# A decoder layer on one core: half of the down-projection pieces of two groups as seven block products in place of eight

## The chip, the core and the metric

The kernel runs on one NeuronCore of a Trainium2 chip. The metric is the device time of one execution in microseconds (us), as the median of several runs.

## What is computed

One hybrid decoder layer on 256 tokens of width 2048, batch 1, all in float32: gated token mixers (latent attention and an RG-LRU recurrence), cross-attention to 256 memory rows, and a convolutional feed-forward block. The change touches the last block:

```python
h = rmsnorm(x, g_pre_ffn[l])
up = causal_dwconv(h @ w_up[l], w_fconv[l], b_fconv[l])
gate, val = jnp.split(up, 2, axis=-1)
x = x + rmsnorm((jax.nn.gelu(gate, approximate=True) * val) @ w_down[l], g_post_ffn[l])
```

`w_up` is 2048 x 11264, `w_down` is 5632 x 2048. The product with `w_down` is the down-projection.

## The kernel before

**Products of float32 by three terms.** Each operand of a large product is split into a high part (rounded to the matmul's format, `fp32r`) and a low part (what is left). A product is then high x high + low x high + high x low, three matmuls (`TERMS`), summed in PSUM. For the weights the split is made on the way: a *piece* of 1 MB (128 partitions x 2048 values) lands by DMA in one of four slots of `raw`; ScalarE copies it to `wsp[.., 0, ..]` (the high part, function `hi`, L1041 to L1054); VectorE subtracts that from `raw` and writes `wsp[.., 1, ..]` (the low part, function `lo`, L1533 to L1540); TensorE waits for the low part (`arrive`). SyncE issues the load of piece c when the low part of piece c-4, the last owner of the `raw` slot, is done (`piece`, L365). ScalarE writes the high part of piece c when TensorE has finished piece c-4, the last owner of the `wsp` slot. ScalarE and VectorE run two pieces ahead of TensorE (`LEAD = 2`): the program text of a phase handles pieces 2 to n+1, so the last two splits are those of the next phase.

**The feed-forward block** is done in three groups of the 44 feature tiles (`GROUPS = [(0, 16), (16, 16), (32, 12)]`). For each group first the up-projection (`PH_UP`), in rounds of two gate and two value tiles (`up_round`), four pieces a round. What TensorE makes there goes through a chain of small operations: ScalarE copies half of it out of PSUM (L1065), VectorE adds the other half (L1548), scales (L2081), two convolution steps (L2086, L2092), ScalarE applies bias and gelu (L1448, L1467), GpSimd multiplies gate and value into `HID` (L2303), ScalarE (L1474) and VectorE (L2122) split that into `hsp`.

Then the down-projection of the group (`PH_DN`, functions `dn_mm` and `dn_y`): one piece is one row tile k of `w_down`, 128 x 2048. TensorE multiplies it with both token halves m and four column quarters b, three terms each, so 24 matmuls of 128 x 512 a piece, into all eight PSUM banks (bank 4m + b). In the first two groups a phase has 16 pieces, 384 matmuls. At its end VectorE moves the eight banks into `y_tok` (L2141 a copy in group 0, L2143 an addition in group 1), and TensorE enters the next up-projection when the first four banks are free (`y_out`). The third group (12 pieces) ends with the norm and the output; it reads `x3_tok`, the residual, which lies in `big_a` from before the first group.

The order of work is written out by hand: each engine has its own program, and the semaphores join them.

## Time and profile before

| | us |
|---|---|
| median of 3 runs | 1735.39 (1735.25 to 1735.74) |
| profiled execution, first to last instruction (span) | 1732.8 |
| TensorE busy in the span | 1724.4 |
| VectorE busy | 1142.9 |
| ScalarE busy | 919.5 |
| GpSimd busy | 157.3 |

The span counts from the first to the last instruction; the time of a run is 2.6 us longer than the span of the profiled execution, for what lies around it. In the rows PE is TensorE's matmul, PEld its weight load, DVE VectorE, ACT ScalarE, POOL GpSimd, SP SyncE; L12 is line 12 of the kernel. The time of one matmul in a group is that of its own way through the pipeline; successive matmuls overlap, so what one adds to the time is the length of a stretch divided by the count.

### The profile page before, as it was taken

To read this page: it belongs to the slowest core of one execution; us is meant where nothing else is said; L and a number is where in the kernel's file an instruction comes from. 1 tells how busy PE (TensorE), PEld (TensorE's weight loads), DVE (VectorE), ACT (ScalarE), POOL (GpSimd) and SP (SyncE) were. 2 spreads that over 40 slices of the span, in tenths; PEclk is the share of its full clock that TensorE was granted. 3 is DMA by queue.
4 is the path that set the end of the run, shared out by engine and by line. 5 is a ranking of instruction groups with operands and counts; after the bars stand their busy time and mean duration, and the time that the engine had idled before them with its cause. 6 is when DMAs were issued, how large, how long until landed. Compare 5 with 4: busy or idle time off the path is not lost.

```text
span 1732.8 us, 25350 instructions
## 1 busy us (share of the span) xinstructions
PE 1724.4 (100%) x8968; PEld 1470.6 (85%) x8968; DVE 1142.9 (66%) x1437; ACT 919.5 (53%) x1175; POOL 157.3 (9%) x183
## 2 busy tenths in 40 slices
PE   9999999999999999999999999999999999999998
PEld 8888888888888888888888888888888888888886
DVE  7766665466788874446566677775467776467766
ACT  7656655443666763344456665553355555245553
POOL 0012210000334520000000000000000000000000
PEclk9999999999999999999999999999999999999999
DMA  9645556566566565556554465556456556545552
GB/s 340 200 141 156 156 196 234 190 237 195 157 193 188 170 242 192 192 187 243 195 177 172 137 194 185 180 179 231 155 185 194 184 181 237 174 151 188 194 213 103
DMA packets 214267, 330.09 MB, mean 190 GB/s; under 512 B 5696, under 2 KB 161984, under 8 KB 206784
## 3 DMA queue, kind: packets, MB, share of 16 engines
q1 hardware_dynamic: 208576, 318.53, 54.5%
q10 hardware_dynamic: 5632, 10.75, 1.7%
q8 instruction: 40, 0.66, 0.2%
q14 instruction: 19, 0.16, 0.0%
HBM read 327.16 MB, written 2.10 MB: 190 GB/s over the span
## 4 chain that ended last, share of the span: by engine, by line
PE 99%; DVE 0%; issue 0%; ACT 0%; DVEq 0%; POOL 0%; POOLq 0%
PE ps L506 51%; PE ps L569 40%; PE ps L522 3%; PE ps L781 1%; PE ps L709 1%; PE ps L631 1%; PE ps L620 0%; PE ps L601 0%; PE ps L738 0%; PE ps L714 0%; PE ps L731 0%; PE ps L625 0%; PE ps L739 0%; PE ps L869 0%; PE ps L853 0%; PE ps L595 0%
## 5 line engine op out<-in xcount | busy, mean ns | idle before, releaser
L1540 DVE TENSOR_TENSOR wsp<-raw,wsp 128x2048 fp32r<-128x2048 f32 (+2 forms) x303 | 671.7, 2235 | 326.3 <-ACT wsp L1054 323.1
L1054 ACT ACTIVATE wsp<-raw 128x2048 fp32r<-128x2048 f32 (+2 forms) x304 | 558.0, 1855 | 284.4 <-PE ps L569 278.1
L506 PE MATMUL ps<-asp,wsp 128*128 128x512 f32 x3064 | 542.4, 339 | 0.0
L506 PEld LDWEIGHTS ps<-asp,wsp 128*128 128x128 f32 x3064 | 469.8, 188 | 70.2 <-DVE asp L2001 0.3
L569 PE MATMUL ps<-wsp,hsp 128*128 128x512 f32 x2292 | 522.9, 389 | 0.0
L569 PEld LDWEIGHTS ps<-wsp,hsp 128*128 128x128 f32 x2292 | 430.0, 188 | 89.0
L506 PE MATMUL ps<-hsp,wsp 128*128 128x512 f32 (+1 forms) x1936 | 349.7, 340 | 0.0
L506 PEld LDWEIGHTS ps<-hsp,wsp 128*128 128x128 f32 x1936 | 297.5, 188 | 42.9
L569 PE MATMUL ps<-wsp,asp 128*128 128x512 f32 x768 | 175.6, 389 | 0.0
L1065 ACT ACTIVATE cr<-ps 128x256 f32<-128x256 f32 x185 | 69.2, 380 | 197.2 <-PE ps L506 180.8
L569 PEld LDWEIGHTS ps<-wsp,asp 128*128 128x128 f32 x768 | 144.0, 188 | 29.8
L2303 POOL TENSOR_TENSOR scr<-scr 128x256 f32<-128x256 f32 x44 | 34.2, 797 | 1003.9 <-DVE scr L2092 1003.9
L1448 ACT ACTIVATE scr<-scr,par 128x256 f32<-128x256 f32 x88 | 48.2, 595 | 60.8 <-DVE scr L2081 60.8
L1548 DVE TENSOR_TENSOR cr<-ps,cr 128x256 f32<-128x256 f32 x88 | 35.1, 418 | 44.4 <-ACT cr L1065 44.4
L2086 DVE SCALAR_TENSOR_TENSOR scr<-scr,par 128x255 f32<-128x255 f32 x88 | 42.5, 484 | 27.4 <-ACT scr L1448 27.2
L2284 POOL TENSOR_TENSOR scr<-scr 128x256 f32<-128x256 f32 x16 | 28.6, 1785 | 246.8 <-ACT scr L1245 246.8
L522 PE MATMUL ps<-wsp,asp 128*128 128x512 f32 (+1 forms) x256 | 47.5, 341 | 0.0
L1474 ACT ACTIVATE hsp<-scr 128x256 f32 (+1 forms) x44 | 18.4, 418 | 53.6 <-POOL scr L2303 53.6
L522 PEld LDWEIGHTS ps<-wsp,asp 128*128 128x128 f32 x256 | 40.0, 188 | 5.8
L2122 DVE TENSOR_TENSOR hsp<-scr,hsp 128x256 f32 (+1 forms) x44 | 18.8, 427 | 36.2 <-ACT hsp L1474 36.2
L1164 ACT ACTIVATE scr<-scr,st 128x128 f32<-128x128 f32 (+1 forms) x32 | 14.3, 449 | 48.3 <-DVE st L1722 48.3
L2092 DVE SCALAR_TENSOR_TENSOR scr<-scr,par 128x254 f32<-128x254 f32 x88 | 38.3, 476 | 0.1
(264 smaller groups left out, 935.6 us busy)
## 6 DMA issues: line engine op xcount, KB each, us to landing
raw<-in_w_up SPq DMA_DIRECT2D x88, 1024.0 KB, 5.6
raw<-in_w_in SPq DMA_DIRECT2D x64, 1024.0 KB, 5.4
raw<-in_w_down SPq DMA_DIRECT2D x44, 1024.0 KB, 5.4
raw<-in_w_in SPq DMA_DIRECT2D x32, 768.0 KB, 4.4
raw<-in_w_o_mla SPq DMA_DIRECT2D x16, 1024.0 KB, 5.0
raw<-in_w_o_lru SPq DMA_DIRECT2D x16, 1024.0 KB, 5.1
raw<-in_w_out SPq DMA_DIRECT2D x16, 1024.0 KB, 5.0
raw<-in_w_ukv SPq DMA_DIRECT2D x8, 1024.0 KB, 5.4
```

What stands on the lines that cost most here:

```text
L506: mm = pe.matmul(ps[:, bank, 0:w], lhs(part, k), x[:, 0:w], start=(f and part == 0), stop=(l and n == 1))
L522: mm = pe.matmul(o, x, r, start=(f and part == 0), stop=(l and n == 1))
L569: mm = pe.matmul(ps[:, bank, :], src[:, k, low * T + m * P:low * T + (m + 1) * P], wsp[:, c, part, cols], start=(first and t == 0), stop=( ...
L1054: act.activation(wsp[:, p0 % SLOTS, 0, 0:n], raw[:, p0 % SLOTS, 0:n], ACT.Copy).then_inc(hi_done, 1)
L1065: act.activation(cr[:, slot, :], ps[:, bank, T:2 * T], ACT.Copy, scale=scale).then_inc(cross_done, 1)
L1448: act.activation(UC[2 * v + e], UR[2 * v + e], ACT.Identity, scale=col(W_F + 2 * P, m), bias=col(B_F, m)).then_inc(up_bias, 1)
L1540: dve.tensor_tensor(wsp[:, slot, 1, 0:n], raw[:, slot, 0:n], wsp[:, slot, 0, 0:n].bitcast(F32), ALU.subtract).then_inc(lo_done, 1)
L1548: return dve.tensor_tensor(dst, ps[:, bank, 0:T], cr[:, slot, :], ALU.add)
L2086: own.mark(dve.scalar_tensor_tensor(out=buf[:, 1:T], in0=src[:, 0:T - 1], scalar=col(W_F + P, m), in1=buf[:, 1:T], op0=ALU.mult, op1=ALU.add))
L2092: dve.scalar_tensor_tensor(out=buf[:, 2:T], in0=src[:, 0:T - 2], scalar=col(W_F, m), in1=buf[:, 2:T], op0=ALU.mult, op1=ALU.add).then_inc( ...
L2284: own.mark(pool.tensor_tensor(IG[e], IG[e], XC[e], ALU.mult))
L2303: pool.tensor_tensor(HID[e], UC[e], UC[2 + e], ALU.mult).then_inc(hid_out, 1)
```

## The change

In the down-projections of the first two groups a piece is now two row tiles (k0, k1) by half of the columns (1024), that is four blocks in order: (k0, b0), (k0, b1), (k1, b0), (k1, b1), each 128 x 512. The phase is two halves h (columns 0 to 1023, then 1024 to 2047), each over the eight pairs of row tiles. Four of the eight pairs stay as they were: a "plain" piece, 24 matmuls. The other four are done by seven block products in place of eight (the Strassen-Winograd form). Each takes two pieces: a "first" piece, loaded by DMA, with three products (9 matmuls), and a "made" piece, not loaded but computed by VectorE from the first, whose four blocks are sums of the first's blocks, with four products (12 matmuls). `DN_HALF` is the order of the twelve pieces of a half.

On the other side four sums of hidden blocks (`forms`) are made for each such pair: GpSimd (`form_sums`) once in every second up round, then split by ScalarE (`form_high`) and VectorE (`form_low`). They lie over `big_a`, so the residual is saved to DRAM in the first group's second round and loaded back ahead of the third group.

The seven products accumulate in PSUM over the four pairs: `q1`, `q6`, `q7`, `q5` in four banks, and the plain ones in the other four, which also take what belongs to one output block alone. At the end of a half ScalarE copies `q1` out (`q1_keep`), VectorE combines the q banks into `y_tok` (`products_out`) and adds the plain banks (`plain_out`). The halves use the two sets of four banks in turn.

The third group is as before, but for a wait on the residual.

```diff
+DN_HALF = [("plain", 0), ("plain", 2), ("first", 1), ("made", 1), ("first", 3), ("made", 3),
+           ("plain", 4), ("first", 5), ("made", 5), ("first", 7), ("made", 7), ("plain", 6)]
...
 SyncE
+                if fn == 16:
+                    for c in range(24):
+                        kind, pair = DN_HALF[c % 12]
+                        if kind != "made":
+                            k, c0 = f0 + 2 * pair, (c // 12) * 1024
+                            piece(dn, 0, c, 2, 1024, w_dn[:, k:k + 2, c0:c0 + 1024])
...
 TensorE
+                        if at == 0 and h == 1:
+                            pe.wait_ge(dn_out, 16 * n + 4)
...
+                        if at == 2 and 2 * n + h:
+                            pe.wait_ge(dn_out, 16 * n + 8 * h)
...
+                        elif kind == "first":
+                            form_mm(q1, block(k0, 0), slot, 1, at == 2, at == 9)
+                            form_mm(dn_plain_bank(h, 0, 1), block(k1, 0), slot, 3, False, False)
+                            mm = form_mm(dn_plain_bank(h, 0, 0), form(pair, 3), slot, 2, False, False)
+                        else:
+                            form_mm(q5, form(pair, 1), slot, 0, at == 3, at == 10)
+                            form_mm(q7, form(pair, 0), slot, 1, at == 3, at == 10)
+                            form_mm(q6, form(pair, 2), slot, 2, at == 3, at == 10)
+                            mm = form_mm(dn_plain_bank(h, 1, 1), block(k1, 1), slot, 3, False, False)
...
 ScalarE
+                def made_high(c):
+                    slot = (dn.p0 + c) % SLOTS
+                    act.wait_ge(gemm_step, dn.g(0, dn.used[c - SLOTS]) if c >= SLOTS else dn.g0)
+                    act.wait_ge(sums_made, dn_sums(n, c) + 1)
+                    act.activation(wsp[:, slot, 0, :], raw[:, slot, :], ACT.Copy).then_inc(hi_done, 1)
...
 VectorE
+                def sums_two(c):
+                    dve.wait_ge(lo_done, dn.p(0, c) + 2 - SLOTS)
+                    dve.wait_ge(landed[(dn.p0 + c) % SLOTS], dn.landed(0, c))
+                    b12 = raw_blocks(c, 0).rearrange("p (a t) -> p a t", a=1).to_broadcast([P, 2, 512])
+                    own.mark(dve.tensor_tensor(raw_blocks(c + 1, 0, 2).rearrange("p (a t) -> p a t", a=2), b12,
+                                               raw_blocks(c, 1, 2).rearrange("p (a t) -> p a t", a=2), ALU.add))
+                def sums_rest(c):
+                    own.wait()
+                    own.link(dve.tensor_tensor(raw_blocks(c + 1, 2), raw_blocks(c + 1, 0), raw_blocks(c, 2), ALU.add))
+                    dve.tensor_tensor(raw_blocks(c + 1, 3), raw_blocks(c + 1, 2), raw_blocks(c, 3), ALU.add).then_inc(sums_made, 1)
...
+                if fn == 16:
+                    form_low(n, 3)
+                    for c in range(LEAD, 24 + LEAD):
+                        kinds = ["plain" if at >= 24 else DN_HALF[at % 12][0] for at in range(c, c + 2)]
+                        if c == LEAD:
+                            sums_two(c)
+                            sums_rest(c)
+                        if kinds[1] == "first":
+                            sums_two(c + 1)
+                        if c == 15:
+                            plain_out(0)
+                        if kinds[0] == "first":
+                            first_low(c)
+                        else:
+                            lo(dn, 0, c)
+                        if kinds[1] == "first":
+                            sums_rest(c + 1)
+                        if c in (13, 25):
+                            products_out(c // 24)
+                        if c == 25:
+                            plain_out(1)
```

How the change moves instructions, at two places. First VectorE at the start of the first down-projection, behind the last up round. Before (L1540 is the low part of a weight piece):

```order
L2122 TENSOR_TENSOR hsp<-scr,hsp 128x256
L351 REGISTER_ALU
L351 COMPARE_AND_BRANCH
L2144 UNCONDITIONAL_BRANCH
L2144 ISA
L1540 TENSOR_TENSOR wsp<-raw,wsp 128x2048 [waits hi_done]
L1538 REGISTER_ALU
L1540 TENSOR_TENSOR wsp<-raw,wsp 128x2048 [waits hi_done]
```

and now (L2213 is `form_low`, L2293, L2299 and L2300 are the weight sums, L2306 the low part of a first piece, L1681 that of a made or plain one):

```order
L2213 TENSOR_TENSOR forms<-scr,forms 128x4x128 [waits fm_hi]
L2293 TENSOR_TENSOR raw<-raw 128x1024 [waits landed2,lo_done]
L2299 TENSOR_TENSOR raw<-raw 128x512 [waits dve_self]
L2300 TENSOR_TENSOR raw<-raw 128x512 [waits dve_self]
L2306 TENSOR_TENSOR wsp<-raw,wsp 128x1536 [waits hi_done]
L2293 TENSOR_TENSOR raw<-raw 128x1024 [waits landed0,lo_done]
L1681 TENSOR_TENSOR wsp<-raw,wsp 128x2048 [waits hi_done]
```

Four operations now stand ahead of the low part of piece 2, and one more ahead of that of piece 3.

Second VectorE around the middle of that phase, between the halves (pieces 10 to 14; L2322 to L2330 are `products_out`):

```order
L1681 TENSOR_TENSOR wsp<-raw,wsp 128x2048 [waits hi_done] x3
L2293 TENSOR_TENSOR raw<-raw 128x1024 [waits landed2,lo_done]
L1681 TENSOR_TENSOR wsp<-raw,wsp 128x2048 [waits hi_done]
L2299 TENSOR_TENSOR raw<-raw 128x512 [waits dve_self]
L2300 TENSOR_TENSOR raw<-raw 128x512 [waits dve_self]
L2322 TENSOR_TENSOR scr<-cols_in,ps 128x512 [waits q1_out,gemm_step]
L2326 TENSOR_TENSOR cols_in<-scr,ps 128x512 [waits dn_out]
L2328 TENSOR_TENSOR cols_in<-ps,scr 128x512
L2330 TENSOR_TENSOR cols_in<-ps,cols_in 128x512 [waits dn_out]
```

and TensorE at the same place (L600 is a plain piece, L1016 a first or made one; the row with `dn_out` is the start of the second half, piece 12):

```order
L1016 MATMUL ps<-wsp,forms 128x512 [waits lo_done]
L1016 MATMUL ps<-wsp,forms 128x512 x8
L1016 MATMUL ps<-wsp,hsp 128x512 x3
L600 MATMUL ps<-wsp,hsp 128x512 [waits hid_lo,lo_done]
L600 MATMUL ps<-wsp,hsp 128x512 x23
L600 MATMUL ps<-wsp,hsp 128x512 [waits dn_out,hid_lo,lo_done]
L600 MATMUL ps<-wsp,hsp 128x512 x23
L600 MATMUL ps<-wsp,hsp 128x512 [waits hid_lo,lo_done]
L600 MATMUL ps<-wsp,hsp 128x512 x23
L1016 MATMUL ps<-wsp,hsp 128x512 [waits fm_lo,dn_out,hid_lo,lo_done]
```

TensorE's piece 12 now stands behind VectorE's fourth operation of `products_out`. Before there was no such wait inside a phase.

## Rows read from the trace of the kernel before

**Rows 1.** Busy time by stage: down 0, up 1, down 1 (stretches of the span)
```profile
core 0: us, PE busy (x) PEld busy (x) DVE busy (x) ACT busy (x) POOL busy (x), PEclk, DMA share, GB/s
...
1170.28:1257.32 87.04, 87.04 (x385) 72.09 (x385) 43.73 (x32) 32.29 (x21) 1.61 (x2) 1.00 0.54 194
1257.32:1437.47 180.15, 180.15 (x1025) 156.68 (x1025) 127.39 (x170) 96.92 (x123) 10.69 (x14) 1.00 0.57 186
1437.47:1524.52 87.05, 87.05 (x386) 72.10 (x385) 43.73 (x32) 32.29 (x21) 1.53 (x2) 1.00 0.54 194
```
**Rows 2.** The chain that ended last: start us, us, what
```profile
1170.28 87.04 PE ps L569 x384
1257.32 180.16 PE ps L506 x1024
1437.47 87.04 PE ps L569 x384
```
**Rows 3.** Groups of instructions of the first down-projection: xcount | busy, mean ns | idle before
```profile
L1540 DVE TENSOR_TENSOR wsp<-raw,wsp 128x2048 fp32r<-128x2048 f32 x16 | 36.1, 2289 | 38.2 <-ACT wsp L1054 38.2
L1054 ACT ACTIVATE wsp<-raw 128x2048 fp32r<-128x2048 f32 x16 | 30.0, 1911 | 47.7 <-PE ps L569 47.7
```
**Rows 4.** Timeline of its start: start us, us, what, [idle before <-releaser]
```profile
1173.99 1.61 POOL L2303 TENSOR_TENSOR scr<-scr 128x256 f32<-128x256 f32 x2 [20.91 <-DVE scr L2092]
...
1176.34 0.42 DVE L2122 TENSOR_TENSOR hsp<-scr,hsp 128x256 f32 x1 [0.27 <-ACT hsp L1474]
1178.08 8.90 DVE L1540 TENSOR_TENSOR wsp<-raw,wsp 128x2048 fp32r<-128x2048 f32 x4 [1.31 <-ACT wsp L1054]
```
**Rows 5.** VectorE groups over the whole span, shapes apart
```profile
L1540 DVE TENSOR_TENSOR wsp<-raw,wsp 128x1536 fp32r<-128x1536 f32 x32 | 55.9, 1765 | 15.4 <-ACT wsp L1054 15.3
...
L2143 DVE TENSOR_TENSOR cols_in<-cols_in,ps 128x512 f32<-128x512 f32 x15 | 10.0, 684 | 5.7 <-PE ps L569 5.5
...
L1772 DVE TENSOR_TENSOR hsp<-scr,hsp 128x512 fp32r<-128x512 f32 x8 | 5.5, 685 | 0.7 <-ACT hsp L1216 0.7
...
L1869 DVE TENSOR_TENSOR big_a<-big_a,scr 128x512 f32<-128x512 f32 x4 | 2.6, 685 | 0.0
...
L2062 DVE TENSOR_TENSOR wsp<-raw,wsp 128x1024 fp32r<-128x1024 f32 x2 | 2.4, 1216 | 0.0
```
**Rows 6.** ScalarE groups over the whole span, shapes apart
```profile
L1054 ACT ACTIVATE wsp<-raw 128x1536 fp32r<-128x1536 f32 x32 | 46.5, 1478 | 0.3
...
L1216 ACT ACTIVATE hsp<-scr 128x512 fp32r<-128x512 f32 x8 | 5.0, 631 | 14.0 <-DVE scr L1782 13.6 <-ACT scr L1207 0.4
```
**Rows 7.** GpSimd groups over the whole span, shapes apart
```profile
L2303 POOL TENSOR_TENSOR scr<-scr 128x256 f32<-128x256 f32 x44 | 34.2, 797 | 1003.9 <-DVE scr L2092 1003.9
...
L2262 POOL TENSOR_TENSOR scr<-scr,st 128x256 f32<-128x256 f32 x16 | 9.8, 614 | 0.0
...
L2262 POOL TENSOR_TENSOR scr<-scr,st 128x128 f32<-128x128 f32 x16 | 6.4, 400 | 91.9 <-DVE st L1726 91.4
```
**Rows 8.** Timeline of VectorE in the tail: two operations each of which waits for the last
```profile
1715.75 0.15 DVE L2184 TENSOR_SCALAR st<-st 128x1 f32<-128x1 f32 x1
...
1716.60 0.15 DVE L2169 RECIPROCAL st<-st 128x1 f32<-128x1 f32 x1
1716.80 0.22 DVE L2170 SCALAR_TENSOR_TENSOR st<-st 128x1 f32<-128x1 f32 x1
```
**Rows 9.** DMA issues: KB each, median us from issue to landing
```profile
raw<-in_w_up SPq DMA_DIRECT2D x88, 1024.0 KB, 5.6
...
raw<-in_w_down SPq DMA_DIRECT2D x44, 1024.0 KB, 5.4
...
raw<-in_w_o_mla SPq DMA_DIRECT2D x16, 1024.0 KB, 5.0
...
raw<-in_w_in SPq DMA_DIRECT2D x4, 576.0 KB, 7.5
```
**Rows 10.** The last stretches of the span, columns as in rows 1
```profile
1726.00:1728.00 2.00, 0.31 (x2) 0.30 (x2) 1.61 (x7) 0.77 (x3) 0.00 (x0) 1.00 0.00 0
1728.00:1730.00 2.00, 0.36 (x2) 0.00 (x0) 1.62 (x3) 0.38 (x1) 0.00 (x0) 0.94 0.63 234
1730.00:1732.00 2.00, 0.00 (x0) 0.00 (x0) 0.00 (x0) 0.00 (x0) 0.00 (x0) 0.50 0.88 291
```
**Rows 11.** Up round ahead of down 0, VectorE's splits: timeline
```profile
1155.58 4.49 DVE L1540 TENSOR_TENSOR wsp<-raw,wsp 128x2048 fp32r<-128x2048 f32 x2 [1.33 <-ACT wsp L1054]
...
1164.25 4.71 DVE L1540 TENSOR_TENSOR wsp<-raw,wsp 128x2048 fp32r<-128x2048 f32 x2 [0.42 <-ACT wsp L1054]
```

More of the change, by code:

```diff
@@ L75, with __init__ @@
 class Phase:
-    def __init__(self, after, trips, ends, crosses=True):
+    def __init__(self, after, trips, ends, crosses=True, made=()):
         self.trips, self.ends, self.n = trips, ends, len(ends)
@@ L96, in __init__ @@
         self.x_end = self.x0 + (self.tiles * trips if crosses else 0)
-        assert self.n % SLOTS == 0
+        self.made = (after.made if after else []) + [self.p0 + c for c in made]
+        assert self.n % SLOTS == 0 and (not made or trips == 1)
     def p(self, i, c):
@@ L111, in landed @@
     def landed(self, i, c):
-        return i * (16 * self.n // SLOTS) + 16 * ((self.p0 + c) // SLOTS + 1)
+        at = self.p0 + c
+        skipped = sum(q < at and q % SLOTS == at % SLOTS for q in self.made)
+        return i * (16 * self.n // SLOTS) + 16 * (at // SLOTS + 1 - skipped)
 class Tally:
@@ L152 @@
     PH_UP.append(Phase(_last, _count // 2, [0, 2, 0, 2]))
-    PH_DN.append(Phase(PH_UP[-1], _count // 4, [0] * 4))
+    if _count % 16 == 0:
+        PH_DN.append(Phase(PH_UP[-1], 1, [0] * 24, made=[c for c in range(24) if DN_HALF[c % 12][0] == "made"]))
+    else:
+        PH_DN.append(Phase(PH_UP[-1], _count // 4, [0] * 4))
     _last = PH_DN[-1]
@@ L237, in build @@
         HID = [s(12), s(13)]
+        FORM = s(8, 2)
+        A11, A21, A12, A22 = (scr[:, 12 * T + n * P:12 * T + (n + 1) * P] for n in range(4))
+        Q1_KEPT, V_SUM, W_SUM = s(14, 2), s(8, 2), cur[:, :]
         landed = [sem(f"landed{n}") for n in range(SLOTS)]
@@ L305, in build, with dn_sums, dn_plain_bank @@
         half = RANK + ROPE
+        def dn_sums(n, c):
+            return 8 * n + 4 * (c // 12) + [e for e in DN_HALF if e[0] == "made"].index(DN_HALF[c % 12])
+        def dn_plain_bank(h, m, b):
+            return 4 * h + 2 * m + b
         def load_cols(eng, n):
@@ L997, in _ @@
                 i, last_ks = dn.trips - 1, range(fn - 4, fn)
[L998 removed]
+                for cs in ((0,), (1,), (2, 3)):
                     for c in cs:
@@ new lines, in _ @@
+                        mm = dn_mm(c, k, 1, b, False, c == 3)
+                    mm.then_inc(dn_done, 1)
+                for h in range(2):
+                    if h:
+                        pe.wait_ge(y_out, 1)
+                    for c, k in enumerate(last_ks):
+                        for t, (part, low) in enumerate(TERMS):
+                            mm = pe.matmul(ps[:, 0 if h else 7, 0:T], hsp[:, k, low * T + P:low * T + 2 * P], wsp[:, c, part, LAST[h]],
+                                           start=(h == 1 and c == 0 and t == 0), stop=(c == 3 and t == 2))
+                    mm.then_inc(dn_done, 1)
@@ new lines, in plain_out @@
+                def plain_out(h):
+                    dve.wait_ge(dn_out, 16 * n + 8 * h + 4)
+                    if n:
+                        own.wait()
+                    for at, (m, b) in enumerate([(0, 0), (0, 1), (1, 0), (1, 1)]):
+                        if at == 3:
+                            dve.wait_ge(gemm_step, dn.g(0, dn.used[12 * h + 11]))
+                        else:
+                            dve.wait_ge(dn_done, 6 * n + 3 * h + at + 1)
+                        y = y_at(h, m, b)
+                        dve.tensor_tensor(y, y, ps[:, dn_plain_bank(h, m, b), :], ALU.add).then_inc(dn_out, 1)
@@ L2293, in _, with form_sums @@
             own.n, own.off = n0 + 6 * PH_LRU.trips, 0
-            for (f0, fn), up in zip(GROUPS, PH_UP):
+            def form_sums(n, pair):
+                pool.wait_ge(hid_out, pair * 4 + 16 * n + 4)
+                if not isinstance(pair, int) or 4 * n + pair:
+                    pool.wait_ge(fm_lo, pair + 4 * n)
+                f7_f5, f6, f3 = (FORM[:, a * P:b * P] for a, b in ((0, 2), (2, 3), (3, 4)))
+                both = scr[:, 12 * T:14 * T].rearrange("p (e t) -> p e t", e=2)
+                own.link(pool.tensor_tensor(f7_f5.rearrange("p (e t) -> p e t", e=2), both[:, 0, :].rearrange("p (e t) -> p e t", e=2),
+                                            both[:, :, P:2 * P], ALU.subtract))
+                own.link(pool.tensor_tensor(f6, FORM[:, P:2 * P], A11, ALU.subtract))
+                pool.tensor_tensor(f3, f6, A12, ALU.add).then_inc(fm_raw, 1)
+            n0 = own.n
+            for n, ((f0, fn), up) in enumerate(zip(GROUPS, PH_UP)):
                 def up_round(i):
```

244 lines of the change are left out of this document (181 added, 63 removed).

## The prediction

> **What bounds the kernel now.** I read the busy time by stage first, then the chain of waits, the groups of the stage, and its timeline. TensorE is busy without a gap through every stage of the feed-forward block, at a granted clock of 1.00, the 2.4 GHz level [rows 1]; the chain that ended last is its matmuls alone [rows 2]. A down-projection takes 87.04 us for 384 matmuls, so 0.2267 us each. VectorE is busy 43.7 of those 87 us, ScalarE 32.3, and both idle only because their `wsp` slot is still in use [rows 1, 3]. So a matmul taken away is worth its 0.2267 us as long as VectorE and ScalarE keep up.
>
> **What TensorE gains.** Per half, four pairs of row tiles go from 24 matmuls to 21. Two halves, two groups: 16 x 3 = 48 fewer, 360 in place of 384 a phase, all of the same shape. 48 x 0.2267 = 10.9 us; a phase needs 81.6 us. A plain piece takes 5.44 us, a first one (9) 2.04, a made one (12) 2.72.
>
> **What VectorE pays.** Prices from rows of the same shapes [rows 3, 5]: low part of 2048 columns 2.29 us, of 1536 1.77; 1024-column sum 1.22; a 512-column addition 0.684, from SBUF or PSUM alike. Of operations that don't wait for each other the next starts 0.065 us before the last one's end (four splits of 2.289 take 8.90 [rows 4]); one that waits for the last starts 0.04 after it [rows 8]. The broadcast operand of the 1024 sum has no row. Bounds: 0.61 us (half the plain row) and 2.29 (twice as many columns); I take the plain 1.22, the nearest.
> A pair costs VectorE 1.22 + 2 x 0.684 + 1.77 + 2.29 = 6.6 us while TensorE works 4.8 on it. Before, two row tiles cost it 4.6 against TensorE's 10.9. A half is four of these, four plain splits and 8 (group 0) or 12 (group 1) additions at its end: 26.6 + 9.2 + 5.5 or 8.2 = 41.3 or 44.0 us, against 40.8 of TensorE. VectorE goes from half idle to as loaded as TensorE, with only two pieces of lead to even out the order. That is the core of the forecast: the gain is eaten unless it never waits, and the order makes it wait.
>
> **The timeline of a phase**, t = 0 where TensorE begins it (1170.28).
> Start. Before, VectorE comes free of the last up round's chain at t = 6.5, starts the low part of piece 2 at 7.8 and ends it near 10.1 [rows 4], 0.8 us ahead of TensorE, which has pieces 0 and 1 until 10.9. Now GpSimd first makes the form sums behind its last product, which ends at 5.3 [rows 4]: 0.80 for 256 columns, and twice 0.52 for 128 (0.797 x 400/614 [rows 7]; bounds 0.40 and 0.80), about 1.9 with the links, so 7.3. ScalarE's split 0.63 [rows 6] and VectorE's 0.685 [rows 5] end at 8.7. Sums for piece 3: 1.22 + 0.68 + 0.68, to 11.3. Low part of piece 2, to 13.0. **TensorE stalls 2.2 us.** VectorE next does the 1024 sum for piece 5 and the low part of 3, to 16.4: stall 1.3, since the first piece kept TensorE only 2.0. Carried on in the same way, with ScalarE's 1.91 and 1.48 [rows 3, 6] ahead of each low part, pieces 4, 5 and 6 wait 0.3, 0.6 and 0.7. Together 5.1 us. Then VectorE has caught up.
> Middle. TensorE ends piece 11, and the half, at 45.9. VectorE ended the low part of 12 at 41.9; the load of piece 14 was issued when the low part of 10 ended (37.5) and lands 5.4 later [rows 9], at 43.0. Sum for 15 to 44.2, low part of 13 to 46.5, two sums to 47.8, and only then the four operations of `products_out`, to 50.4. TensorE's piece 12 waits for the fourth: **stall 4.6 us**, though the q banks were complete when piece 10 ended at 40.5. ScalarE's copy of q1 (one 512-column copy, done by 42.9) is not the last. In group 1 `products_out` has one more operation ahead of that count: 5.1.
> Second half. VectorE's two sets of additions and splits end before TensorE needs them: plain pieces 12 and 13 give it 10.9 us. No stall; `products_out` at the end falls beside the last plain piece and ends at 90.9, TensorE at 91.3. In group 1 it ends last, 0.2 us late.
> Phase 0: 81.6 + 5.1 + 4.6 = 91.3, 4.2 more than 87.04. Phase 1: 81.6 + 5.1 + 5.1 + 0.2 = 92.0, 5.0 more. **Sum +9.2 us.**
>
> **A rule against a row.** Operations that wait for the one before start 0.04 us after it and those that don't 0.065 before its end, so I charge 0.1 us per link [rows 4, 8]. The Trainium skill (VectorE: DVE Perf Modes, The DRAIN you can't avoid) says that a semaphore between two VectorE operations costs nothing extra. By that the sum would be +7.8; the rows are of this kernel, so +9.2 stands.
>
> **The rest at nothing.** Up rounds: three of eight in a group take on 0.63 us of ScalarE and 0.69 of VectorE. The low part of the next round's piece 0 ends near 1166.5 and that of piece 1 at 1169.0 [rows 11], against 1170.3 and 5.6 us later: cover of 3.8 and 6.9 us; without it each round would cost up to 0.7. GpSimd is nearly idle there. Residual saved and reloaded: 2 MB each beside 4 MB of weights a round at a DMA share of 0.57 [rows 1]; a late weight load would have to lose the two pieces of lead. ScalarE's wait for the end of phase 1 ahead of the reload holds back piece 2 of the next round by the length of TensorE's last piece, to about t + 5 of the 11 us it has. SyncE issues 16 loads a phase as before, each of the same size, the made pieces none. At the end of a phase VectorE's last plain additions stand ahead of the low part of piece 2 of the up-projection: ready at 95.7 (98.6 in group 1), needed at 102.5.
>
> The profiled execution's span of 1732.8 lies 2.6 below the median shown; that part is not touched. 1735.4 + 9.2 = **1744.6 us**.
>
> **Rivals.**
> *VectorE is cheap enough: faster.* The stalls rest on the sums being at full price. If the 16 small sums and 8 large ones of a phase cost nothing beside the other work, the same timeline gives 82.6 and 83.0: 8.5 us faster, 1726.9. If they cost half, 85.5 and 86.0, 2.5 faster, 1732.9. It decides where they fall below about half of their rows. For it: a broadcast operand has no row, and additions could be shorter when one input is read twice. Against: 512 columns cost 0.684 in every row, whatever the operands, and 1024 cost 1.216 [rows 5]. 6 in 100.
> *VectorE doesn't wait between: no change.* Even at the row prices, with all of VectorE's waits gone, its own chain from 8.0 on ends `products_out` at 85.7 in group 0 and 88.8 in group 1, so -1.3 and +1.8: +0.5, 1735.9. For that the lead would have to be more than two pieces. With prices a little low as well it stays within the bound: 9 in 100.
> *The clock falls in the stalls.* In the tail TensorE works 0.7 of 4 us and the granted clock falls from 1.00 to 0.50, the 1.2 GHz level, around 1730 [rows 10]. The stalls of 4.6 and 5.1 us come behind dense work, and the second half has no slack to hide slow matmuls: piece 12 at the half clock costs up to 5.4 more. Half of that, twice: +5.4, 1750.0. Against: 12 and 13 are plain, and no row shows a gap of this length between dense stretches. 13 in 100. The Trainium skill (TensorE: Matmul & The Clock Gate, Why this matters for your kernels) warns that idle gaps between bursts of matmuls bring the lower clock; that is this rival's rule.
> *Loads land late.* A first piece's load must be down before its sums, and it is issued only when the low part four pieces earlier is done. At 6.5 us to landing in place of 5.4 the timeline gives +16.6, 1752.0; at 5.0, +8.2. For it: two row tiles by 1024 are shorter lines than before. Against: the up weights with still shorter lines land in 5.6 [rows 9], which gives +10.2. 6 in 100.
>
> **How the numbers follow.** The forecast as worked out has 66 in 100; with the clock and the loads slower has 85. About 0.2% (3.5 us) is what a measurement of this kernel can tell from no change. The form sums' bounds (7.3 give or take 0.4) move it by 0.7 to 0.9, the broadcast sum at 0.684 gives +3.7, and at 2.29 +24.8, which I leave out as the sum has 1024 results. The range goes from 1738.0, where splits and additions are all a tenth cheaper (the timeline then gives +3.0), to 1752.0, late loads or two full slow pieces.
>
> **What would show it.** Right: TensorE idle behind VectorE's low part before pieces 2 and 3 of each phase, about 2 and 1.3 us, and 4 to 5 us at the middle behind L2330 (group 1: its counterpart); 48 matmuls fewer; VectorE busy over 80 us in a phase of 91 or 92. Wrong: a phase below 87 us, a 1024 sum far from 1.22 us, a granted clock below 1.00 in a phase, or a stall at another piece of over 2 us.

## The result, and the profile after

The changed kernel takes 1748.97 us (median of 4 runs, 1748.25 to 1749.44), the kernel before it 1735.32 in the same comparison: a ratio of 1.0078, 95% interval 1.0064 to 1.0093, so 13.7 us slower. The forecast was 1744.6, the range 1738.0 to 1752.0.

The profiled execution has a span of 1747.2 us against 1732.8, and all but 0.3 us of the difference lies in the two changed down-projections. Busy time in each of them, columns as in [rows 1]:

```profile
1170.51:1265.27 94.76, 86.06 (x361) 69.01 (x361) 81.15 (x71) 45.64 (x32) 3.59 (x5) 0.96 0.55 189
```
```profile
1445.45:1538.85 93.40, 86.05 (x360) 68.99 (x360) 83.72 (x76) 45.63 (x32) 3.43 (x5) 0.96 0.57 192
```

Against [rows 1], where each took 87.04: 24 matmuls a phase are gone, VectorE is busy 81 and 84 us in place of 44, TensorE is idle for 8.7 and 7.4 us, and its granted clock is 0.96 in place of 1.00. So two things ate the 5.4 us a phase that the matmuls were worth, and more: idle time, and matmuls that became slower. The timeline of TensorE in the first of the two shows where (start us, us, instructions, in brackets the idle time before them and its releaser):

```profile
1170.34 11.04 PE L600 MATMUL ps<-wsp,hsp 128*128 128x512 f32 x48
1183.73 1.66 PE L1016 MATMUL ps<-wsp,hsp 128*128 128x512 f32 x6 [2.35 <-DVE wsp L2306]
...
1187.07 2.35 PE L1016 MATMUL ps<-wsp,forms 128*128 128x512 f32 x9 [1.00 <-DVE wsp L1681]
...
1196.08 5.74 PE L600 MATMUL ps<-wsp,hsp 128*128 128x512 f32 x24 [0.32 <-DVE wsp L1681]
...
1221.46 13.89 PE L600 MATMUL ps<-wsp,hsp 128*128 128x512 f32 x48 [4.69 <-DVE cols_in L2330]
```

The stalls lie where the forecast had put them: ahead of the first few pieces, and ahead of piece 12, with which the second half begins. The row to stop at is that of the 48 matmuls behind the long one. The same 48 take 11.04 us at the phase's start and 13.89 here. The granted clock (third column from the right) says why; windows around that place:

```profile
1216.00:1220.00 4.00, 0.78 (x4) 0.31 (x2) 3.93 (x5) 1.11 (x1) 0.00 (x0) 1.00 0.18 75
1220.00:1221.40 1.40, 0.00 (x0) 0.00 (x0) 1.40 (x4) 0.80 (x1) 0.00 (x0) 0.66 0.00 0
1221.40:1226.00 4.60, 4.54 (x11) 3.60 (x12) 4.60 (x6) 0.00 (x0) 0.00 (x0) 0.50 0.39 124
1226.00:1227.00 1.00, 1.00 (x4) 0.81 (x3) 1.00 (x2) 0.00 (x0) 0.00 (x0) 0.50 1.00 410
...
1228.00:1265.00 37.00, 37.00 (x165) 30.52 (x164) 30.43 (x24) 18.29 (x11) 0.00 (x0) 1.00 0.66 218
```

The clock goes from 1.00 to 0.50, the 1.2 GHz level, while TensorE stands still, stays there for over five us of work that can't be hidden behind anything, and is back by 1228. In the second phase the 48 matmuls take 12.76 us. There the clock is still at 1.00 when TensorE starts again, falls 0.9 us later and stays low for some 3.4 us:

```profile
1496.03 12.76 PE L600 MATMUL ps<-wsp,hsp 128*128 128x512 f32 x48 [4.29 <-DVE cols_in L2333]
```
```profile
1496.00:1496.90 0.90, 0.87 (x4) 0.76 (x5) 0.90 (x2) 0.00 (x0) 0.00 (x0) 1.00 0.00 0
1496.90:1500.00 3.10, 3.10 (x9) 2.42 (x8) 3.10 (x4) 0.00 (x0) 0.00 (x0) 0.50 0.00 0
```

VectorE in the first phase, the groups that answer to [rows 3] and [rows 5]:

```profile
L1681 DVE TENSOR_TENSOR wsp<-raw,wsp 128x2048 fp32r<-128x2048 f32 x16 | 36.3, 2286 | 5.7 <-ACT wsp L1595 5.2 <-ACT wsp L1144 0.5
L2306 DVE TENSOR_TENSOR wsp<-raw,wsp 128x1536 fp32r<-128x1536 f32 x8 | 14.0, 1751 | 1.4 <-ACT wsp L1602 1.4
L2293 DVE TENSOR_TENSOR raw<-raw 128x1024 f32<-128x1024 f32 x8 | 9.7, 1219 | 1.6 <-DMA raw<-in_w_down 1.6
L2300 DVE TENSOR_TENSOR raw<-raw 128x512 f32<-128x512 f32 x8 | 5.5, 692 | 0.3
L2299 DVE TENSOR_TENSOR raw<-raw 128x512 f32<-128x512 f32 x8 | 5.5, 684 | 0.0
```

Every price is the forecast's within 20 ns, the broadcast sum (1219 ns against the 1.22 taken) among them. And VectorE around the middle, in order:

```profile
1214.04 1.23 DVE L2293 TENSOR_TENSOR raw<-raw 128x1024 f32<-128x1024 f32 x1 [1.62 <-DMA raw<-in_w_down]
1215.19 2.29 DVE L1681 TENSOR_TENSOR wsp<-raw,wsp 128x2048 fp32r<-128x2048 f32 x1
1217.39 0.68 DVE L2299 TENSOR_TENSOR raw<-raw 128x512 f32<-128x512 f32 x1
1218.11 0.69 DVE L2300 TENSOR_TENSOR raw<-raw 128x512 f32<-128x512 f32 x1
1218.71 0.68 DVE L2322 TENSOR_TENSOR scr<-cols_in,ps 128x512 f32<-128x512 f32 x1
1219.43 0.69 DVE L2326 TENSOR_TENSOR cols_in<-scr,ps 128x512 f32<-128x512 f32 x1
1220.04 0.68 DVE L2328 TENSOR_TENSOR cols_in<-ps,scr 128x512 f32<-128x512 f32 x1
1220.64 0.68 DVE L2330 TENSOR_TENSOR cols_in<-ps,cols_in 128x512 f32<-128x512 f32 x1
```

It waits for the load of piece 14, and TensorE, which needs only `products_out` (L2322 to L2330), waits behind three weight sums (L2293, L2299, L2300) and a split (L1681) that are for pieces 13 and 15.

### The profile page after: what moved, and what is told of

Its sections match the earlier page's. It is cut to its first block, busy times and chain, and to the rows that moved or that the text cites. A ratio compares the mean times of both kernels' runs of the same rounds, so it can differ in the third digit from the quotient of the medians.

```text
span 1747.2 us, 25073 instructions
## 1 busy us (share of the span) xinstructions
PE 1722.4 (99%) x8920; PEld 1464.4 (84%) x8920; DVE 1228.1 (70%) x1533; ACT 948.6 (54%) x1203; POOL 172.8 (10%) x207
## 4 chain that ended last, share of the span: by engine, by line
PE 85%; issue 5%; DVE 5%; ACT 2%; DMA 1%; POOL 1%; ACTq 0%; DVEq 0%; POOLq 0%; SPq 0%
PE ps L537 43%; PE ps L600 33%; PE ps L553 3%; PE ps L1016 2%; DVE wsp L1681 2%; ACT wsp L1144 1%; PE ps L812 1%; DVE raw L2293 1%; PE ps L740 1%; PE ps L662 1%; DMA raw<-in_w_down 1%; ACT wsp L1595 0%; PE ps L632 0%; PE ps L769 0%; PE ps L745 0%
## 5 line engine op out<-in xcount | busy, mean ns | idle before, releaser
L1681 DVE TENSOR_TENSOR wsp<-raw,wsp 128x2048 fp32r<-128x2048 f32 (+2 forms) x303 | 672.4, 2235 | 257.9 <-ACT wsp L1144 245.8
L1144 ACT ACTIVATE wsp<-raw 128x2048 fp32r<-128x2048 f32 (+2 forms) x288 | 528.8, 1852 | 198.3 <-PE ps L600 186.1
L600 PE MATMUL ps<-wsp,hsp 128*128 128x512 f32 x1908 | 442.4, 392 | 9.6 <-DVE cols_in L2330 4.7
L600 PEld LDWEIGHTS ps<-wsp,hsp 128*128 128x128 f32 x1908 | 360.6, 189 | 86.4 <-issue 9.8
L600 PE MATMUL ps<-wsp,asp 128*128 128x512 f32 x768 | 175.6, 389 | 0.0
L600 PEld LDWEIGHTS ps<-wsp,asp 128*128 128x128 f32 x768 | 144.0, 188 | 29.8
L1595 ACT ACTIVATE wsp<-raw 128x2048 fp32r<-128x2048 f32 x16 | 30.7, 1917 | 50.2 <-DVE raw L2300 42.3
L1016 PE MATMUL ps<-wsp,forms 128*128 128x512 f32 x192 | 48.0, 397 | 1.6 <-DVE wsp L1681 1.6
L1016 PEld LDWEIGHTS ps<-wsp,forms 128*128 128x128 f32 x192 | 36.4, 192 | 10.8 <-DVE wsp L1681 3.2
```

Of the source, the lines that this page charges most:

```text
L600: mm = pe.matmul(ps[:, bank, :], src[:, k, low * T + m * P:low * T + (m + 1) * P], wsp[:, c, part, cols], start=(first and t == 0), stop=( ...
L1016: mm = pe.matmul(ps[:, bank, :], lhs(low), wsp[:, slot, part, quarter(block)], start=(first and t == 0), stop=(last and t == 2))
L1144: act.activation(wsp[:, p0 % SLOTS, 0, 0:n], raw[:, p0 % SLOTS, 0:n], ACT.Copy).then_inc(hi_done, 1)
L1595: act.activation(wsp[:, slot, 0, :], raw[:, slot, :], ACT.Copy).then_inc(hi_done, 1)
L1681: dve.tensor_tensor(wsp[:, slot, 1, 0:n], raw[:, slot, 0:n], wsp[:, slot, 0, 0:n].bitcast(F32), ALU.subtract).then_inc(lo_done, 1)
```

## The experiments

Two theories were open. **A**: VectorE's order makes the idle time, and the idle time lowers the clock. **B**: the clock falls for another reason, and the candidate is the burst of loads beside the slow matmuls (DMA share 1.00 at 1226). The rows above already speak against B: the clock is falling from 1220 to 1221.4, and is low from 1496.9 to 1500, with a DMA share of 0.00. Beside them stood the question of what in VectorE's work is to blame: the order, the sums, or the sheer load. All ratios are against the kernel before, run on the same chip (1735.0 to 1735.2).

### The stall filled with matmuls (e1_warm)

```diff
                         if at == 0 and h == 1:
+                            pe.wait_ge(q1_out, 2 * n + 1)
+                            for _ in range(19):
+                                pe.matmul(ps[:, 4, :], hsp[:, 0, 0:P], wsp[:, slot, 0, 0:512], start=True, stop=True)
                             pe.wait_ge(dn_out, 16 * n + 4)
```

> The changed kernel, with 19 idle matmuls (128 x 512, into PSUM bank 4, which nobody uses then) on TensorE in the middle of each of the two phases, where piece 12 waits for products_out. They take 19 x 0.2267 = 4.3 us of the 4.7 and 4.3 us stall. Theory A (the granted clock falls because TensorE stands idle in the middle stall, and the slow matmuls of pieces 12 and 13 cost 3.0 and 1.9 us): granted clock 1.00 throughout both phases, the 48 matmuls after the stall in 10.9 to 11.1 us in place of 13.9 and 12.8, the kernel about 4.5 us faster than the changed one, 1744.5. Rival B (the slow matmuls come from the burst of weight loads, DMA share 1.00 at 410 GB/s, that falls on the same microseconds, and not from the idle time): the 48 matmuls still take 13 to 14 us in the first phase, time unchanged at 1749.

Measured: 1746.78 us (1745.68 to 1747.12), ratio 1.0067 (1.0053 to 1.0081), 2.2 less than the changed kernel. In the profile the middle of the first phase is

```profile
1216.86 4.47 PE L1043 MATMUL ps<-wsp,hsp 128*128 128x512 f32 x19
1221.74 11.19 PE L600 MATMUL ps<-wsp,hsp 128*128 128x512 f32 x48 [0.41 <-DVE cols_in L2333]
```

and the granted clock there, with the burst of loads in the second line:

```profile
1221.40:1226.00 4.60, 4.26 (x19) 3.52 (x20) 4.60 (x6) 0.00 (x0) 0.00 (x0) 1.00 0.28 78
1226.00:1227.00 1.00, 1.00 (x6) 0.84 (x5) 1.00 (x3) 0.00 (x0) 0.00 (x0) 1.00 1.02 422
```

In the first phase `products_out` ends when it did before: piece 12 starts 51.14 us after the phase's first matmul, 51.12 in the changed kernel. The loads come as before, and the clock stays at 1.00. **B falls.** The 48 matmuls take 11.19 and, in the second phase, 11.17 us, so the fall of the clock had cost 13.89 - 11.19 = 2.7 and 12.76 - 11.17 = 1.6 us, 4.3 together.

The profiled span fell by 3.3 and the median by 2.2, where 4.5 was expected. One part is the load of piece 14 in the second phase. VectorE waits longer for it, first the changed kernel, then this one:

```profile
1488.14 1.23 DVE L2293 TENSOR_TENSOR raw<-raw 128x1024 f32<-128x1024 f32 x1 [0.75 <-DMA raw<-in_w_down]
```
```profile
1486.40 1.22 DVE L2296 TENSOR_TENSOR raw<-raw 128x1024 f32<-128x1024 f32 x1 [1.37 <-DMA raw<-in_w_down]
```

and piece 12 starts at 51.28 in place of 50.75 us after the first matmul there. Another 0.3 is lost ahead of the first phase. The clock also fell once behind the stall at the start of the first phase (0.50 from 1186 to 1188), but that cost nothing: piece 6 starts 25.73 us after the first matmul, 25.74 in the changed kernel. The rest, and the other 1.1 between the profiled run (the fastest of the five) and the median, is not traced.

### The weight sums left out (e2_nosums)

`sums_two` and `sums_rest` are not issued; ScalarE waits for the first piece's landing instead. The made pieces are split from what lies in their slots, so this kernel does not compute the sums of weight blocks.

> The changed kernel with the weight sums on VectorE left out: a made piece takes what lies in its raw slot. TensorE, ScalarE and the DMA queues do the same work as in the changed kernel; 24 operations of VectorE a phase are gone (21 us). Theory A (VectorE's added work in its order makes the stalls): phases of 82.4 us in place of 94.8 and 93.4, no stall over 1 us, granted clock 1.00, 1735.3 - 9.4 = 1726, the gain of 48 matmuls nearly whole. Rival C (the split of first and made pieces, the shorter DMA lines or the two halves with their PSUM hand-over cost TensorE by themselves): stalls of over 1 us stay at pieces 3 to 6 or 12, and the time stays above 1731.

Measured: 1726.92 us (1726.71 to 1728.85), ratio 0.9956 (0.9942 to 0.9969). The phases take 82.7 and 82.8 us, and at the middle nothing is left:

```profile
1207.14 16.48 PE L600 MATMUL ps<-wsp,hsp 128*128 128x512 f32 x72
```

Piece 11 and the two plain pieces behind it are one run of 72 matmuls. So without 2.6 us of VectorE work per pair the whole gain of 48 matmuls is there but for 1.2 us a phase. Rival C (the new shape of the pieces costs TensorE by itself) falls. It is VectorE's work that eats the gain; whether by its order or by its load this run does not tell.

### products_out one piece earlier (e3_early)

```diff
-                        if c in (13, 25):
-                            products_out(c // 24)
+                        if c in (12, 25):
+                            products_out(c // 24)
```
and the same for ScalarE's `q1_keep`.

> The changed kernel with products_out of the first half (and ScalarE's copy of q1 ahead of it) one place earlier in the order: behind the low part of piece 12, ahead of the 1024 sum for 15, the low part of 13 and two sums. The same operations, only the order differs. Theory A: the middle stall of 4.7 and 4.3 us goes wholly (VectorE is free at t = 41.9, ends the fourth operation at 44.7, TensorE ends piece 11 at 45.9 plus 0.7), and with it the low clock and its 3.0 and 1.9 us. Some comes back: the sums and low parts of the second half are late by what TensorE is early, up to 1 us at the end of phase 0 and 3.9 us over phase 1. Phases 87.7 and 90.6 (87.04 before), plus 0.5 for the start as measured: 1740. Rival D (the stall only moves: piece 13 or 14 waits as long for its low part instead): TensorE idle 4 us at 13 to 15, clock still falls, 1748.

Measured: 1739.56 us (1738.96 to 1739.82), ratio 1.0025 (1.0015 to 1.0035), 9.4 less than the changed kernel: two stalls of 4.3 to 4.7 us and the 4.3 of the clock are gone, and part comes back, most of it at the end of the phases. Rival D, that the stall only moves, falls.

```profile
1211.37 16.48 PE L600 MATMUL ps<-wsp,hsp 128*128 128x512 f32 x72
...
1258.26 180.34 PE L537 MATMUL ps<-asp,wsp 128*128 128x512 f32 x1024 [0.49 <-DVE cols_in L2330]
```
```profile
1528.96 51.39 PE L537 MATMUL ps<-asp,wsp 128*128 128x512 f32 x291 [1.62 <-DVE cols_in L2333]
```

The first half no longer gives VectorE a rest, so the second ends with `products_out` late by 0.5 and 1.6 us, and the second phase has two stalls of 0.3 us on the way there.

### The last form split behind the start (e4_start)

```diff
-                    form_low(n, 3)
                     for c in range(LEAD, 24 + LEAD):
+                        if c == 6:
+                            form_low(n, 3)
```
and ScalarE's `form_high` at c == 3.

> The changed kernel with the last form_high and form_low of each group (the split of the fourth form, needed first by piece 9) moved behind the start: ScalarE does it after the high part of piece 2, VectorE after the low part of 5. Theory A (at the start VectorE waits 1.6 us for GpSimd's form sums and ScalarE's split, ahead of the sums for piece 3): stall at piece 2 goes from 2.5 us to about 0.3, of which 0.7 comes back at piece 6, 1.5 us a phase gained, the middle stall and the clock fall unchanged: 1749.0 - 3.1 = 1745.9. Rival E (VectorE is the bound of the whole first half, so what is won at piece 2 is lost at 3 to 6 and in the middle): time within 1 us of 1749.0.

Measured: 1746.46 us (1745.67 to 1749.2), ratio 1.0068 (1.0054 to 1.0082), 2.5 less than the changed kernel by the medians. But the five runs lie apart: 1745.67, 1746.39 and 1746.46 with a mean granted clock of 0.997, and 1748.56 and 1749.20 with 0.995 and 0.994. The profile is of the run of 1748.56, so it shows one of the two longer ones:

```profile
1182.53 1.66 PE L1016 MATMUL ps<-wsp,hsp 128*128 128x512 f32 x6 [0.51 <-DVE wsp L2307]
...
1195.47 5.78 PE L600 MATMUL ps<-wsp,hsp 128*128 128x512 f32 x24 [0.92 <-DVE wsp L1682]
...
1221.45 13.38 PE L600 MATMUL ps<-wsp,hsp 128*128 128x512 f32 x48 [5.25 <-DVE cols_in L2331]
```

The first stall goes from 2.35 to 0.51 us, but the one at piece 6 grows from 0.32 to 0.92 and the one in the middle from 4.69 to 5.25: VectorE's work was moved, not taken away, and a part of it shows again at the next place where TensorE needs it. Even so piece 12 starts 0.6 us earlier in its phase than in the changed kernel, and 1.2 earlier in the second phase, where the clock takes 0.7 of it back: the 48 matmuls behind the stall take 13.46 us there in place of 12.76. Theory A named 1745.9 and rival E a time within 1 us of 1749.0; three runs lie near the one and two near the other, so this edit decides less than its median says.

### Both, and the second half too (e5_order)

> Edit: both changes of order together, and the second of them at both halves' ends: the last form split of ScalarE and of VectorE is moved behind the start of the down-projection (as in the run with the form split moved), and products_out with ScalarE's copy of q1 stands one piece earlier at both ends of a half (as in the run with it moved, which did so for the first half only). No work is added or taken away. Theory (VectorE's order makes the stalls; its load of 41 to 44 us per half against TensorE's 40.8 is what is left): the timeline gives phases of 86.1 and 86.2 us, 0.9 less than 87.04 each, so -1.9 and, by how the two runs apart came out 0.5 above their timelines, 1734 us, a ratio of 0.998 to 1.000; no idle of TensorE over 1.5 us in a phase and a granted clock of 1.00 in the middle. If the two gains only add up as the two runs measured them (-9.4 and -2.5 from 1749.0): 1737. Rival (VectorE's load itself is the bound, whatever the order): the stalls go to the end of the phases and the time stays near that of the run with products_out moved, 1739.5. A time under 1730 would say that the down-projections can get most of the 10.9 us per phase back, which neither expects.

Measured: 1734.61 us (1733.77 to 1735.22), ratio 0.9997 (0.9988 to 1.0006): 14.4 us below the changed kernel and no different from the kernel before. The phases take 85.8 and 87.5 us. In group 0 all that is left are four stalls of 0.3 to 1.0 us near the start; group 1 has two more, of 0.3 us each, in its second half, the later of them

```profile
1503.05 5.73 PE L600 MATMUL ps<-wsp,hsp 128*128 128x512 f32 x24 [0.30 <-DVE wsp L1682]
```

The two runs apart had brought 9.4 and 2.5; here it is 14.4, but this kernel also has `products_out` early at the end of the second half, which neither had, so the runs don't show how the three add up. The rival that the load alone sets the time (1739.5) falls. For group 1, though, where the forecast counted 44.0 us of VectorE work in a half of 40.8, the phase came out 1.3 above its timeline. The count itself was somewhat high: two halves of 44.0 are more than the 87.5 us that the phase took. It adds up durations of which successive ones overlap.

### The weight sums on GpSimd (e6_pool)

```diff
+                            pool.tensor_tensor(y[:, 0:512], x[:, 0:512], x[:, 512:1024], ALU.add).then_inc(ps_a, 1)
+                            pool.tensor_tensor(y[:, 512:1024], x[:, 0:512], x[:, 1024:1536], ALU.add)
...
+                            pool.tensor_tensor(y[:, 1024:1536], y[:, 0:512], x[:, 1024:1536], ALU.add).then_inc(ps_b, 1)
...
+                            pool.tensor_tensor(y[:, 1536:2048], y[:, 1024:1536], x[:, 1536:2048], ALU.add).then_inc(sums_made, 1)
```

> Edit: the order of the run before this one, and all weight sums of the pairs made by GpSimd in place of VectorE, as four additions of 512 columns each (the 1024-column one in two). VectorE keeps splits, additions of products and stores. SyncE also waits for the sums before it reloads a first piece's slot. Theory (what costs is VectorE's 2.6 us of sums per pair, and GpSimd is nearly idle in a down-projection): it turns on GpSimd's price for 512 columns, which no row has. The nearest are 0.99 us and 0.80 for 256 columns with other work beside it. Linear in columns that is 1.6 to 2.0 per addition, 6.4 to 8 us per pair, more than the 4.8 us that TensorE needs per pair but about the 10.9 / 2 = 5.4 that a half has per piece slot (four pairs in 40.8 us, 10.2 each on average, three of them close together): the timeline gives -5.4 us (1730) at 4 us per pair, +2.8 (1738) at 6 us, and well over 1745 at 8 us. If VectorE's own operations beside it become longer (the two share what they read and write), splits of 2.29 us at over 2.4, then slower still. I expect 1745 or more. Rival (GpSimd's price is mostly fixed, so 512 columns take about 1 us): 1730.

Measured: 1775.91 us (1774.35 to 1777.84), ratio 1.0239 (1.0225 to 1.0253). The groups of the first phase, GpSimd and then VectorE:

```profile
L2566 POOL TENSOR_TENSOR raw<-raw 128x512 f32<-128x512 f32 x8 | 22.0, 2744 | 0.0
L2563 POOL TENSOR_TENSOR raw<-raw 128x512 f32<-128x512 f32 x8 | 18.5, 2312 | 0.0
L2568 POOL TENSOR_TENSOR raw<-raw 128x512 f32<-128x512 f32 x8 | 17.8, 2223 | 0.6
L2562 POOL TENSOR_TENSOR raw<-raw 128x512 f32<-128x512 f32 x8 | 13.4, 1669 | 12.7 <-DMA raw<-in_w_down 12.7
```
```profile
L1685 DVE TENSOR_TENSOR wsp<-raw,wsp 128x2048 fp32r<-128x2048 f32 x16 | 40.9, 2574 | 28.1 <-ACT wsp L1598 26.9 <-ACT wsp L1147 1.2
L2310 DVE TENSOR_TENSOR wsp<-raw,wsp 128x1536 fp32r<-128x1536 f32 x8 | 21.6, 2701 | 0.7 <-ACT wsp L1605 0.7
```

Four additions take (22.0 + 18.5 + 17.8 + 13.4) / 8 = 9.0 us per pair, and VectorE's own splits grew from 1.75 to 2.70 and from 2.29 to 2.57 us. The means hide two prices. The timeline near the start has both:

```profile
1182.18 1.29 POOL L2566 TENSOR_TENSOR raw<-raw 128x512 f32<-128x512 f32 x1
...
1186.85 2.56 DVE L1685 TENSOR_TENSOR wsp<-raw,wsp 128x2048 fp32r<-128x2048 f32 x1 [7.01 <-ACT wsp L1598]
1187.22 3.32 POOL L2566 TENSOR_TENSOR raw<-raw 128x512 f32<-128x512 f32 x1
1189.34 2.83 DVE L2310 TENSOR_TENSOR wsp<-raw,wsp 128x1536 fp32r<-128x1536 f32 x1
```

Alone, an addition of 512 columns takes GpSimd 1.29 us, so the sums of a pair would be some 5.2; begun while VectorE is splitting, the same one takes 3.32, 2.03 more. The Trainium skill (SBUF — State Buffer, SBUF: two separate sides) has VectorE operations with two SBUF inputs and GpSimd's take turns at a shared pair of ports, each holding it for a whole instruction; the rows agree with that: GpSimd's addition ends at 1190.54, 1.13 us behind VectorE's split (1189.41), and VectorE's next split ends 1.63 us behind that addition. The clock falls here too, to 0.50 behind eight of the stalls. TensorE waits up to 5.89 us for a made piece here. Expected was 1745 or more, so the direction was right and the size far off: the expectation had 6.4 to 8 us per pair from rows of 256 columns and no number for what the two engines do to each other.

### Two pairs per half in place of four (e7_two, e9_twoasis)

```diff
-DN_HALF = [("plain", 0), ("plain", 2), ("first", 1), ("made", 1), ("first", 3), ("made", 3),
-           ("plain", 4), ("first", 5), ("made", 5), ("first", 7), ("made", 7), ("plain", 6)]
+DN_HALF = [("plain", 0), ("plain", 2), ("first", 1), ("made", 1), ("plain", 3), ("plain", 4),
+           ("first", 5), ("made", 5), ("plain", 6), ("plain", 7)]
```

with the order of e5_order:

> Edit: the order of the run e5_order, and two pairs per half made as seven products in place of four: a half is P0, P2, F1, M1, P3, P4, F5, M5, P6, P7 (P plain, F first, M made). 372 matmuls per phase, 24 fewer in all than before the change in place of 48. Theory (a pair is worth it while VectorE has slack: 6.6 us of VectorE per pair against 4.8 of TensorE, but two plain tiles cost it 4.6 against 10.9): VectorE has 13.2 + 18.4 + 5.5 or 8.2 = 37.1 to 39.8 us a half against TensorE's 42.2, so it no longer is the bound; the timeline gives phases of 84.9 us (372 x 0.2267 = 84.3 and 0.6 of start), 2.1 less than 87.04 each: 1731 us, ratio 0.9976, faster than the kernel before by more than can be mistaken. Rival (stalls come from how the pieces stand to each other, not from VectorE's load): the phases stay at 86 or more and the time at 1734 to 1736, as with four pairs in this order. Expected of the granted clock: 1.00 throughout both phases.

and with the order of the changed kernel:

> Edit: two pairs per half as in e7_two, but with the order of the changed kernel (last form split ahead of the start, products_out one piece later). It parts the number of pairs from the order. Theory (with two pairs per half VectorE has about 39 us of work against TensorE's 42.2, so products_out no longer stands in anyone's way, wherever it is, while the form split at the start still does): the timeline gives 87.1 us for each phase, +0.1 for the sum, with TensorE idle before piece 2 by over 2 us and nothing in the middle; e7_two came out 1.6 above its timeline, so 1735.3 to 1737, a ratio of 1.000 to 1.001. Granted clock 1.00 behind the middle, where nothing idles. Rival (the order at the middle matters with two pairs as it does with four): an idle of 2 us or more at the middle of a phase and a fall of the clock behind it, 1740 or more.

Measured: e7_two 1732.53 us (1732.09 to 1733.28), ratio 0.9986 (0.9977 to 0.9995), **faster than both kernels** (by 2.6 us against the one before, less than the 3.5 us named ahead of the result, but its 11 runs give an interval that ends below 1); e9_twoasis 1737.40 (1736.58 to 1739.24), ratio 1.0015 (1.0006 to 1.0024). First phase of e7_two, its two stalls and the way from there:

```profile
1182.08 1.66 PE L1017 MATMUL ps<-wsp,hsp 128*128 128x512 f32 x6 [0.50 <-DVE wsp L2308]
...
1184.74 2.35 PE L1017 MATMUL ps<-wsp,forms 128*128 128x512 f32 x9 [0.31 <-DVE wsp L1683]
...
1203.26 21.92 PE L601 MATMUL ps<-wsp,hsp 128*128 128x512 f32 x96
```

Its phases take 85.8 us each, 84.3 of matmuls and 1.5 of stalls and refills, where the expectation had 0.6 (84.9 a phase, 1731); four pairs per half have 81.6 of matmuls and end at 85.8 and 87.5. In e9_twoasis the middle is as clean, and only the start differs:

```profile
1183.42 1.66 PE L1017 MATMUL ps<-wsp,hsp 128*128 128x512 f32 x6 [2.35 <-DVE wsp L2307]
```
```profile
1451.24 2.40 PE L1017 MATMUL ps<-wsp,hsp 128*128 128x512 f32 x6 [2.38 <-DVE wsp L2307]
1453.43 3.77 PE L1017 MATMUL ps<-wsp,forms 128*128 128x512 f32 x12
```

So the rival that the middle is decided by the order with any number of pairs falls: with two pairs VectorE is through with everything before TensorE asks for it, late `products_out` or not. And the order alone is worth 4.9 us here (some 0.9 of it through the clock), against 14.4 with four pairs. Its time is 0.4 above the most that was expected: behind one of its two stalls of 2.35 us the clock fell, as the slow matmuls of the last fence show (12 in 3.77 us against 2.88), behind the other it didn't.

The phases of all kernels, in us, from the timelines (each from the start of the first matmul of the phase to that of the first of the next up-projection; where a stall ends the phase this is 0.2 more than a stretch that begins at the end of the matmul before, as in the rows above). The profiled run of e1 is 1.1 us below its median, that of e4 2.1 above:

| kernel | phase 0 | phase 1 | time | ratio |
|---|---|---|---|---|
| before | 87.0 | 87.0 | 1735.2 | 1 |
| changed | 94.8 | 93.6 | 1749.0 | 1.0078 |
| e1 stall filled | 92.2 | 92.4 | 1746.8 | 1.0067 |
| e2 no weight sums | 82.7 | 82.8 | 1726.9 | 0.9956 |
| e3 products_out early | 87.7 | 90.5 | 1739.6 | 1.0025 |
| e4 form split moved | 93.7 | 93.0 | 1746.5 | 1.0068 |
| e5 both, both halves | 85.8 | 87.5 | 1734.6 | 0.9997 |
| e6 sums on GpSimd | 106.1 | 107.2 | 1775.9 | 1.0239 |
| e7 two pairs, order of e5 | 85.8 | 85.8 | 1732.5 | 0.9986 |
| e9 two pairs, order kept | 87.6 | 88.6 | 1737.4 | 1.0015 |

## Why the prediction was right, and where it was short

The sign and the reason were right, and the time lies within the range, 4.4 us above the forecast. By its own steps:

**TensorE's gain.** 360 matmuls a phase, 48 fewer: as stated (8920 in place of 8968). e2_nosums shows that they are worth it when VectorE keeps up.

**VectorE's prices.** All of them held. The broadcast operand, which had no row before, costs the full 1.22 us; the rival that the sums are cheap (6 in 100) was about this and fell. e2_nosums gave 1726.9, the very time that this rival named for sums at nothing.

**The start.** Forecast: stalls of 2.2, 1.3, 0.3, 0.6 and 0.7, 5.1 in all. Measured: 2.35 ahead of piece 2, 1.3 ahead of piece 3 (by the starts of the pieces; the bracket shows 1.00), 5.2 in all until piece 6 starts, and 5.5 by the end of piece 11, at 46.3 us where 45.9 was forecast. The form sums took GpSimd 0.99, 0.52 and 0.46 us where 0.80 and twice 0.52 were taken.

**The middle.** Forecast 4.6 and 5.1, measured 4.7 and 4.3. Counted from the phase's start, piece 12 begins at 50.95 and 50.58 us, forecast 50.5 and 51.0. The two errors have one cause and opposite signs: the load of piece 14, on which VectorE waits there (the first line of its timeline), took 5.90 us in the first phase and 5.03 in the second, where 5.4 was taken for both:

```profile
1208.05 5.90 DMA raw<-in_w_down
```
```profile
1483.01 5.03 DMA raw<-in_w_down
```

That is +0.5 and -0.4, just what piece 12 is off by.

**The second half.** Forecast: no stall. Right, and the 0.2 at the end of group 1 came as 0.14 of idle time. But the forecast had it run at full clock, and here is **the step that failed**: the clock's fall behind the middle stall stood as a rival with 13 in 100, at 5.4 us, and belonged into the sum. It cost 4.3 us (e1_warm), and 9.2 + 4.3 = 13.5 is near the 13.7 that was measured; the phases of the profiled execution grew by 14.1, the other 0.6 being the load's 0.1 and 0.5 of smaller losses behind the stalls. The evidence against it was "no row shows a gap of this length between dense stretches", which says only that the kernel before had none; the rows that there were, of the tail [rows 10], showed the fall. That 2.7 in the first phase is just the half of piece 12's loss that the rival took is luck: no piece bounds the slow stretch, which lasted 5.8 us in one phase and 3.4 in the other. The Trainium skill (TensorE: Matmul & The Clock Gate, Why this matters for your kernels) gave the warning; the trace agrees, with 4.3 to 5.3 us of idle time ahead of each of four such falls (two here, two in e4_start), and none in the middle where the gap was filled or gone.

**The rule against a row.** The Trainium skill (VectorE: DVE Perf Modes, The DRAIN you can't avoid) has a semaphore between two VectorE operations cost nothing extra, measured there on eight copies. In the timeline of the middle the operations that wait for the last one start 0.04 us after its end (L2300 at 1218.11 behind L2299's 1218.07, L2326 at 1219.43 behind 1219.39), and those that don't wait for it start 0.08 to 0.09 before it (L2322, L2328). So the row's 0.1 us per link was right to charge.

**No waits left** (the rival of no change). e5_order is close to that case, by a change of order and not by more lead: 1734.6 where the rival named 1735.9.

**Loads late.** 5.9 us once, 5.0 the other time: neither the 6.5 of this rival nor a lasting change.

What stays open: why the clock falls behind some stalls of 2.35 us and not behind others of the same length in the same kernel (one phase of two in the changed kernel, in e1_warm and in e9_twoasis, both in e3_early), and why it fell in the stall of one phase and behind that of the other. No run was made for it. Also not tried: three pairs per half, whose pieces don't come out even with the four slots.

## What to carry to other kernels

When an algebraic saving moves work from the bound engine to its feeder, price a unit of it on both (here 4.8 us of TensorE against 6.6 of VectorE per pair), and take only as many units as the feeder has slack for: half as many pairs were better (0.9986) than all of them in the same order (0.9997). Then look at what each consumer's wait is queued behind on the feeder, above all at a hand-over where buffers are passed on: the same work in another order was worth 14.4 us, more than the saving itself. And a stall of over 4 us of TensorE behind dense work is to be costed with the slow matmuls behind it, here up to 2.7 us each.
